# Attention of a two-layer encoder in fp32: the order of two steps of TensorE inside the loop over query tiles

## The reference

```
def dense_bidir_attention(q, k, v):
    s = einsum('bqhgd,bkhd->bhgqk', qb, k) * scale
    p = softmax(s, axis=-1)
    return einsum('bhgqk,bkhd->bqhgd', p, v)

layer 0: multi-head latent attention, 4 heads, q and k of 192, v of 128   (+ a short gated convolution)
layer 1: grouped-query attention, 8 query heads, 2 key/value heads of 128
each layer: h = h + mixer(rms_norm(h));  h = h + swiglu(rms_norm(h))      (hidden size 2816)
```

## Time and profile before

| | us |
|---|---|
| median of 3 runs | 2430.07 (2429.94 to 2430.51) |
| profiled execution, its own time | 2430.68 |
| its span | 2428.9 |
| TensorE busy | 2330.0 (96% of the span) |
| VectorE / ScalarE / GpSimd busy | 1265.3 / 915.3 / 1229.5 |
| mean granted clock of TensorE | 0.984 of full speed |

### The profile page before, as it was taken

One profiled execution on the slowest core, in us unless ns is written; L12 is line 12 of the kernel. 1 busy time (PEld: TensorE's weight loads), 2 busy tenths in 40 slices (PEclk: granted clock), 3 DMA queues, 4 the chain that ended last, 5 costly groups with the idle time before them and its releaser, 6 DMA issues. The chain is left out here.

```text
span 2428.9 us, 37774 instructions
## 1 busy us (share of the span) xinstructions
PE 2330.0 (96%) x14683; PEld 2124.9 (87%) x14683; DVE 1265.3 (52%) x2049; ACT 915.3 (38%) x1927; POOL 1229.5 (51%) x997
## 2 busy tenths in 40 slices
PE   7999979899999999999998998989999999999998
PEld 7998878899899999999997887888878888888886
DVE  5221377537644444444448468864864444444444
ACT  5124556535322222222225346664532222222221
POOL 1343348544655555555543336764455555555551
PEclk9999989999999999999998999999999999999999
DMA  5131100422111111111112100013211111111111
GB/s 200 45 122 44 40 1 1 160 87 79 57 53 53 49 53 49 49 46 42 53 36 79 34 2 1 1 53 92 79 52 52 52 52 52 53 52 53 53 52 74
DMA packets 186209, 137.20 MB, mean 56 GB/s; under 512 B 7217, under 2 KB 175938, under 8 KB 186034
## 3 DMA queue, kind: packets, MB, share of 16 engines
q1 hardware_dynamic: 185904, 134.71, 17.9%
q10 hardware_dynamic: 130, 0.09, 0.0%
HBM read 121.63 MB, written 12.85 MB: 55 GB/s over the span
## 5 line engine op out<-in xcount | busy, mean ns | idle before, releaser
L2247 POOL TENSOR_TENSOR w_lo<-stage,w_hi 128x512 fp32r<-128x512 f32 x384 | 517.1, 1351 | 638.0 <-ACT w_hi L2148 635.7
L2148 ACT ACTIVATE w_hi<-stage 128x512 fp32r<-128x512 f32 x384 | 239.3, 628 | 585.4 <-PE PS L170 582.8
L2456 DVE TENSOR_TENSOR hT<-hT,PS 128x528 f32<-128x528 f32 (+1 forms) x384 | 266.8, 695 | 335.2 <-PE PS L170 333.8
L168 PE MATMUL PS<-x_hi,w_lo 128*128 128x264 f32 (+2 forms) x1152 | 374.4, 325 | 12.9 <-POOL w_lo L2247 6.8
L169 PE MATMUL PS<-x_lo,w_hi 128*128 128x264 f32 (+2 forms) x1152 | 371.9, 323 | 0.0
L170 PE MATMUL PS<-x_hi,w_hi 128*128 128x264 f32 (+2 forms) x1152 | 371.6, 323 | 0.0
L168 PE MATMUL PS<-s_hi,w_lo 128*128 128x264 f32 (+1 forms) x1104 | 353.4, 320 | 3.1 <-DVE s_lo L2410 3.1
L170 PE MATMUL PS<-s_hi,w_hi 128*128 128x264 f32 (+1 forms) x1104 | 353.9, 321 | 0.0
L169 PE MATMUL PS<-s_lo,w_hi 128*128 128x264 f32 (+1 forms) x1104 | 352.7, 320 | 0.0
L168 PE MATMUL PS<-b_hi,w_lo 128*128 128x264 f32 (+1 forms) x864 | 279.4, 323 | 4.3 <-POOL w_lo L2247 4.3
L169 PE MATMUL PS<-b_lo,w_hi 128*128 128x264 f32 (+1 forms) x864 | 278.9, 323 | 0.0
(11 more groups left out here) (318 smaller groups left out, 4906.8 us busy)
## 6 DMA issues: line engine op xcount, KB each, us to landing
stage<-in_ffn_w SPq DMA_DIRECT2D x280, 256.0 KB, 2.8
stage<-in_even_w_out SPq DMA_DIRECT2D x32, 256.0 KB, 2.7
stage<-in_odd_w_out SPq DMA_DIRECT2D x32, 256.0 KB, 2.6
stage<-in_mla_w_in SPq DMA_DIRECT2D x12, 512.0 KB, 6.3
stage<-in_gqa_w_qkv SPq DMA_DIRECT2D x12, 512.0 KB, 3.6
h_spill<-hT SPq DMA_DIRECT2D x8, 528.0 KB, 5.1
hT<-h_spill SPq DMA_DIRECT2D x8, 528.0 KB, 6.7
conv_hi<-s_hi SPq DMA_DIRECT2D x4, 528.0 KB, 2.7
```

The lines of the kernel that those rows point to most:

```text
L168: T.matmul(out, a_lo, b_hi, start=first, stop=False)
L2148: A.activation(ring(w_hi, n), source(n), ACT.Copy).then_inc(rounded, 1)
L2247: G.tensor_tensor(ring(w_lo, n), source(n), ring(w_hi, n).bitcast(F32), ALU.subtract).then_inc(split, 1)
L2456: V.tensor_tensor(o, o, sums(st.slot), ALU.add).then_inc(drained, 1)
```

## The change

In TensorE's loop the scores of tile n+1 are issued ahead of the transposes of tile n-2, instead of behind them. Nothing else changes, and both attentions use this loop.

```diff
                     scores(0)
                     for n in range(len(tiles) + lag + 3):
+                        if n + 1 < len(tiles):
+                            scores(n + 1)
                         if lag <= n < len(tiles) + lag:
                             turn_probs(n - lag)
-                        if n + 1 < len(tiles):
-                            scores(n + 1)
                         for what in items_at.get(n, []):
                             prepare(what)
```

## The result

| | before | after |
|---|---|---|
| median of the runs, us | 2430.29 (2429.94 to 2431.96, 4 runs) | 2474.98 (2474.33 to 2479.53, 4 runs) |
| profiled execution, us | 2430.68 | 2474.47 |
| its span, us | 2428.9 | 2472.7 |

The changed kernel is slower: the ratio is 1.0185 with a 95% interval of 1.0173 to 1.0197, that is 44.7 us. The forecast was 2470, with a range of 2452 to 2492.

A forecast was written before the change was run, and what follows sets the result against it. TensorE was taken to bound the attentions. Layer 1's +28.6 and layer 0's +11.1 us, first tiles at nothing, made +39.7 on the profiled 2430.7: 2470 us, range 2452 to 2492, at 80%.

The forecast's parts named there:

- The ring: Transposes(n-2), ScalarE's rounding, exponentials(n), scores(n+2) wait in turn; shortest iteration 2.89 us in layer 1, 3.18 in layer 0.
- Layer 1: Attention of layer 1, tiles 7 to 63: 166.1 us in place of 137.5, +28.6 us.
- The iteration of 2.89 us: Layer 1, 53 iterations: scores 0.81, transposes 0.46 and delay up to the next scores 1.62 us, one behind the other.
- the one with the tail item: Three iterations of layer 1 whose extra item waits for VectorE's low part of the tile just turned: 4.3 us each.
- Layer 0: Attention of layer 0: 17.1 us per five-tile unit against 15.65, +7.3 for five units; with the last six tiles +11.1 us.
- The last six tiles: End of layer 0's attention, without items: six iterations of 3.18 us, 19.1 against 15.25, +3.8 us.
- The first tiles: Eight intervals in layer 0, seven in layer 1: costed at nothing, existing waits being longer; 5 us either way.
- Rival 1, the clock: Short idles lower TensorE's clock in the attentions: 2506 us if for a quarter of the tiles, 2488 for an eighth; 9%.
- Rival 2, a gain: ScalarE's order does not close the chain; scores cover the transposes' wait for GpSimd, gaining up to 22.2 us; 5%.
- Rival 3, no change: TensorE, 93 to 95% busy, doesn't mind its order; delay hides behind items and output: 2430 us, 5 around it; 6%.
- Signs named in advance: Layer 1: nearly every scores group waits for exponentials, some 60 us in all; exponentials start 2.9 us apart, 3.2 in layer 0.

## Why the prediction was right

The forecast, +39.7 us, stood against +43.8 us of the profiled executions. The ring, its length and its place were foreseen; that the sums agree to 1 us in layer 1 is in part luck. Point by point:

- **Layer 1.** Between the exponentials of tiles 7 and 63, at 1494.45 and 1661.11 us:

```profile
1494.45 0.70 ACT L1732 ACTIVATE gain_rows<-PS,stat 128x528 f32<-128x528 f32 x1
...
1661.11 0.70 ACT L1732 ACTIVATE tmp<-PS,stat 128x528 f32<-128x528 f32 x1 [0.30 <-DVE stat L1904]
```

  166.7 us against 166.1 in the sum and 137.5 before. The iteration of 2.89 us measured 2.90 to 2.93 (+1.4 in all), the one with the tail item 4.45 instead of 4.3 (+0.4), and the last of all 1.64 (-1.2), which the sum had not seen: there are no further scores between the last transposes. These misses cancel. The iteration with the tail item took 4.44 us before, too, so the change cost nothing there.
- **Layer 0.** The five units from tile 8 to 33 took 456.92 - 371.45 = 85.5 us: 17.1 each, the sum's number, with 3.86 us at j = 2 instead of 4.0 and 0.03 to 0.05 more in each of the other four. The last six tiles took 17.7 us and not 19.1, for the same reason as in layer 1: +2.5 in place of +3.8.
- **The first tiles**, costed at nothing, cost 1.8 us in layer 0 and 3.5 in layer 1. This is the step that was off. It went by "longer than the new ones", said of the waits there, and that overlooked what the low clock behind those waits does to a ring (at 1.2 GHz the round took 4.13 us) and that the ring already holds ahead of tile 7. At 5.3 us together it is just over the bound of 5 us that the text gave.
- **The rest**, -0.4 in all, lies around: -0.35 ahead of the first exponentials of layer 0, -1.0 from its last ones to the output projection, -0.4 from there to the first ones of layer 1, and +1.4 behind its last ones. Their causes are open.
- **Rival 1, the clock**, did not come past the first tiles: the granted clock is 1.00 from 1494 to 1662 us, with idle times of up to 1.0 us in a round. The rule of the Trainium skill ("TensorE: Matmul & The Clock Gate", section "A second HAM failure mode: psum-queue depth-cycling") does not show in the changed kernel. With the output moved ahead too the trace agrees with it: the clock swings, and stood at 0.74 to 0.87 over 40 us.
- **Rival 2, a gain:** the waits of L1825 for GpSimd did go, from 22.2 us to 5.8:

```profile
  POOL rope L1670: 4.4, 5
...
  POOL tmp L1670: 1.1, 2
  POOL gain_rows L1670: 0.3, 1
```

  16 us of waiting left, and 45 came. The two were never of one kind: the first was a wait in a few iterations, the second is in every one.
- **Rival 3, no change**, did not come either: TensorE, busy 93 to 95% before, was idle 2.8 and 4.0 us more in the 40 us of the two stretches.
- **Signs named in advance.** Scores wait for exponentials in three of four iterations of layer 1 and 64 times in all, 46.9 us at the weight load where some 60 were foreseen. That the matmuls' own list shows 23 us, and puts another 20 us of layer 1 down to VectorE, was not. Of these, 10.2 are scores that waited for the exponentials, and 9.8 are the first chunk of the output, which waits for VectorE's low part of the output before it; it does so inside the delay of the ring. At j = 0 the new idle time is split in two, 0.78 us ahead of the output and 0.19 ahead of the scores.

What the experiments add: the loss grows by the length of a copy put into the ring (26.8 us for 28) where the old order takes half of that; half of the scores give back more than half of it; and the two attentions add up. That the ring runs through ScalarE's order is supported by the first of these. The direct test, the exchange on ScalarE, closed another ring, and so does not show how the changed kernel would run without this one; no run here opens the ring and wins the 45 us back.

## What to carry to other kernels

In a pipeline of several engines, write down for each engine the order of its own steps and look for rings: a path of waits that leads back to the same engine one iteration later. The pace can't be faster than a ring's length over its iterations. What an engine does between the two ends of a ring is cover. Here scores(n+1) stood between the transposes and the scores(n+2) that wait for them; moving them ahead of the transposes took the cover away though no work was added. A busy share of 93% does not make an order safe to change, and opening one ring by a swap on another engine is apt to close the next.

## What was not expected of the hardware

In the changed kernel the granted clock stayed at its full level from 1494 to 1662 us, with TensorE idle for up to 1.0 us in a round of 2.9 us. With the second copy on ScalarE it stayed there too, from 1508 to 1668 us, with idle times of up to 1.5 us in a round of 3.4 us. With the output moved ahead it fell and rose several times in layer 1 with idle times of up to 1.37 us, and for 23 us it did not. So in these traces the length of TensorE's idle times does not tell by itself whether the clock falls.

One delay was the same to 0.01 us at each place read: from the start of the exponentials of 528 columns to the scores that waited for them 0.84 us, at full clock (1539.72 to 1540.56, 1542.64 to 1543.48) and where TensorE was at half (1479.61 to 1480.45). So TensorE's clock does not enter into it.
